# Retention heads: query, gate, key, gate as the order of the next head's first products, and the key groups moved with it

## The chip, the cores and the metric

The program runs on one core of one Trainium2 chip. The metric is the device time of one execution in microseconds (us). The kernel before took 2175.74 us, the median of three runs (2175.48 to 2181.7). The execution that the profiler recorded took 2178.27 us, of which 2176.5 us are the span of the trace.

## What is computed

The reference is one step of a decoder layer for 1024 prompt tokens and 8 sample tokens. The change touches only the part that does two things at once: the four retention heads of both groups, and the attention of the sample tokens over a paged cache of 4096 past tokens each.

```python
rq, rk, rv, rg, fq, fk, fv, ff, ga, gb = jnp.split(x @ w_in, offsets, axis=-1)
rq = rotary(rq.reshape(b, t, RET_HEADS, RET_DK), pos)
rk = rotary(rk.reshape(b, t, RET_HEADS, RET_DK), pos) * (RET_DK ** -0.5)
...
# per retention head, chunk by chunk (rq, rk, rv -> o, state)
inner = jnp.einsum('bihd,bjhd->bhij', qc, kc) * intra
o = einsum(inner, vc) + einsum(qc * q_decay, s)
...
rn = group_norm(ret_o) * gn_w + gn_b
u_a = (jax.nn.silu(rg) * rn) @ w_pa
merged = jax.nn.sigmoid(ga) * u_a + jax.nn.sigmoid(gb) * u_b
...
# sample tokens: softmax(q . k_past + bias) . v_past over 32 pages of 128 rows per token
```

## The kernel before

**Products.** One head needs ten products of the 1032 token columns with 128 columns of `w_in`: rotated query (rq), rotated key (rk), two gate tiles (ga), two value tiles (rv), two further gate tiles (gb) and two tiles of rg. They are numbered w = 0 to 9; `COLS` and `STEP` (L774, L775) give each its columns. A product (L108 to L126) has three chunks of 344 tokens, one PSUM bank each (banks 0, 1, 2), and a chunk is 24 matmuls: eight k-tiles times three terms, since weight and x are split in a high and a low part. TensorE starts a chunk only when the chunk of the product before it has been read out of its bank (`bank_free`), and starts a product only when its weight has been split: ScalarE makes the high part (L97), VectorE the low part (L104), and GpSimd reloads the raw weight slot after that (L89). There are two weight slots.

**Heads.** The first four products of head 0 stand before the loop (the opening). Products 4 to 9 of a head stand in its body, and at its end follow the first four products of the next head, called 10 to 13 here (the transition). There are three transitions. The head-to-head order of every engine is written out by hand.

**Who empties the banks.** A rotation (`rotate`, L1259 to L1270) is VectorE's: it reads the chunk's bank three times and writes `rq_t` or `rk_t`; it uses the two tiles `rot_cos` and `rot_sin`. A gate (`gate_chunk`, L1072 to L1079) is ScalarE's: a sigmoid from the bank into a tile `sg`, which is `rot_cos` or `rot_sin` again, and a store of 172 KB to DRAM. So gates wait until the rotations are through (L1085, L1177). The silu of rg (L1102) writes six buffers `silus`: the same two tiles and, for the other four, halves of `inner_t` and `q_decayed_t`. VectorE multiplies them into the normed output (L1376, six "gated products"), and ScalarE stores that (L1106).

**The cache stream.** While the heads run, the sample attention goes through 8 tokens, each with 16 groups of two pages of keys (VectorE: a multiply, L1199, and a reduction, L1203) and 16 groups of values (TensorE: 16 small matmuls, L913). Keys and values have four slots of 512 KB each. SyncE issues all loads in one fixed order, key group i of one token and then value group i of the token before, four such pairs to a pass of a loop; at the start of a pass it fetches the page numbers of the whole pass into registers. It issues key group i only when VectorE has reduced group i - 4 of that slot, and value group i only when TensorE has used group i - 4. The tables `VALUES_...` and `KEYS_...` (L691 to L700) say how many groups each engine takes at each place; `VALUES_B` and `KEYS_B` belong to the stretch from the norm to the end of the transition. After its last group a token goes through `cache_max`, a maximum over partitions on GpSimd, `cache_shift` (L1224), exp (L1070), and at the end `cache_tail` (L920, L924) on TensorE, `cache_norm` (L1232, L1234) on VectorE, `cache_turn` (L930) on TensorE and `cache_out`.

## Time and profile before

| | |
|---|---|
| median of the runs | 2175.74 us |
| the profiled execution | 2178.27 us, span 2176.5 us |
| the four heads, with opening and cache attention | about 370 to 1081 us |
| opening (first four products, first sample token's keys) | 372 to 428 us |
| first, second, third transition (products 10 to 13) | 544.51 to 609.80, 720.39 to 784.11, 894.38 to 957.76 us |
| TensorE busy, whole span | 1999.7 us (92%) |
| VectorE busy, whole span | 1158.6 us (53%) |

Times of rows are us from the start of the span, and durations are us unless marked ns. A row of the timeline has start, duration, engine, line, operation, output and inputs; in brackets stands how long the engine was idle before it and what it waited for. "SPq" rows are loads being issued by SyncE, one for both pages of a group (x2).

### The profile page before, as it was taken

What the parts mean: (1) busy time and instruction counts of PE and PEld (TensorE: products, weight loads), DVE (VectorE), ACT (ScalarE), POOL (GpSimd) and SP (SyncE); (2) the same over time, 40 slices, a digit from 0 to 9 for tenths busy, and PEclk for the clock granted to TensorE, in tenths of its full rate; (3) what the DMA queues carried; (4) which work ended last, traced back from release to release, by engine and by line L of the source; (5) the groups of instructions that cost most, each with busy time, mean ns of one, the idle gap of its engine ahead of it and who ended that gap; (6) DMA issues with size and microseconds to landing.
All of it is one profiled execution on the core that took longest, in us unless ns stands there. A gap on an engine that the chain in (4) does not pass through costs nothing.

```text
span 2176.5 us, 39095 instructions
## 1 busy us (share of the span) xinstructions
PE 1999.7 (92%) x14335; PEld 1868.4 (86%) x14335; DVE 1158.6 (53%) x1771; ACT 647.7 (30%) x1178; POOL 216.3 (10%) x253
## 2 busy tenths in 40 slices
PE   7998998898899799799798999799999999999996
PEld 5896887887798698698688898699999999999996
DVE  3654454967856866876332865733322333233348
ACT  4444443134123123223311101444301332123224
POOL 1000000020010020020000100400000001000004
PEclk9998999999899899899889999899999999999999
DMA  3211102597887877787742411111111111111154
GB/s 119 67 36 44 39 20 92 191 315 248 272 296 248 267 263 269 258 291 240 229 147 94 121 49 29 30 48 39 49 48 49 48 39 49 48 49 39 42 150 129
DMA packets 152256, 277.55 MB, mean 128 GB/s; under 512 B 19105, under 2 KB 58398, under 8 KB 152118
## 3 DMA queue, kind: packets, MB, share of 16 engines
q1 hardware_dynamic: 116114, 175.78, 24.3%
q0 software_dynamic: 23232, 82.80, 12.9%
q10 hardware_dynamic: 12800, 17.40, 2.2%
q8 instruction: 80, 1.31, 0.2%
q14 instruction: 30, 0.25, 0.0%
HBM read 247.77 MB, written 28.25 MB: 127 GB/s over the span
## 4 chain that ended last, share of the span: by engine, by line
PE 43%; DVE 5%; DMA 1%; issue 1%; ACT 1%; DVEq 0%; SPq 0%; ACTq 0%
PE bank L121 39%; PE bank L1624 3%; DVE x_lo L1845 1%; DMA gated_raw<-gated_t_scratch 1%; DVE chunk_tmp L1774 0%; DVE chunk_tmp L1776 0%; DVE z L1842 0%; PE banks L1582 0%; DVE merged_hi L1778 0%; DVE moving_lo L1780 0%; DVE w_lo L1915 0%; DMA tail_raw<-in_w_down_dram 0%; DVE y L1891 0%; DMA z<-fox_t_scratch 0%; PE banks L1610 0%
## 5 line engine op out<-in xcount | busy, mean ns | idle before, releaser
L121 PE MATMUL bank<-x_hi,w_hi 128*128 128x344 f32 (+1 forms) x1944 | 642.6, 331 | 55.1 <-DVE rot_sin L1267 25.2
L121 PE MATMUL bank<-x_lo,w_hi 128*128 128x344 f32 (+1 forms) x1944 | 632.2, 325 | 0.0
L121 PE MATMUL bank<-x_hi,w_lo 128*128 128x344 f32 (+1 forms) x1944 | 631.9, 325 | 0.0
L121 PEld LDWEIGHTS bank<-x_hi,w_hi 128*128 128x128 f32 (+1 forms) x1944 | 373.0, 192 | 73.7 <-issue 62.9
L121 PEld LDWEIGHTS bank<-x_lo,w_hi 128*128 128x128 f32 (+1 forms) x1944 | 372.8, 192 | 1.6
L121 PEld LDWEIGHTS bank<-x_hi,w_lo 128*128 128x128 f32 (+1 forms) x1944 | 372.7, 192 | 1.7
L97 ACT ACTIVATE w_hi<-w_raw 128x1024 fp32r<-128x1024 f32 (+3 forms) x139 | 141.7, 1022 | 550.1 <-PE bank L121 372.4
L121 PE MATMUL bank<-moving_hi,w_hi 128*128 128x344 f32 x744 | 229.8, 331 | 25.8 <-DVE moving_lo L1756 14.1
L121 PE MATMUL bank<-moving_lo,w_hi 128*128 128x344 f32 x744 | 239.6, 322 | 0.0
L104 DVE TENSOR_TENSOR w_lo<-w_raw,w_hi 128x1024 fp32r<-128x1024 f32 (+3 forms) x139 | 164.4, 1183 | 117.1 <-ACT w_hi L97 115.8
L121 PE MATMUL bank<-moving_hi,w_lo 128*128 128x344 f32 x648 | 210.0, 324 | 0.0
L1199 DVE TENSOR_TENSOR cache_keys<-cache_keys,q_wide 128x1024 f32<-128x1024 f32 x128 | 156.1, 1221 | 39.0 <-DMA cache_keys<-in_cache_k_dram 39.0
L121 PEld LDWEIGHTS bank<-moving_hi,w_hi 128*128 128x128 f32 x744 | 139.0, 192 | 35.3 <-issue 16.4
L1203 DVE TENSOR_REDUCE score<-cache_keys 128x16 f32<-128x1024 f32 x128 | 154.9, 1211 | 0.0
L121 PEld LDWEIGHTS bank<-moving_lo,w_hi 128*128 128x128 f32 x744 | 141.4, 190 | 0.1
L138 PE MATMUL bank<-x_hi,w_hi 128*128 128x344 f32 x384 | 138.0, 359 | 2.3 <-DVE rv_rows L1366 2.3
L1859 DVE SCALAR_TENSOR_TENSOR stage<-stage,conv_cols_tile 128x1024 f32<-128x1024 f32 x22 | 28.3, 1285 | 186.0 <-ACT stage L1699 186.0
L121 PEld LDWEIGHTS bank<-moving_hi,w_lo 128*128 128x128 f32 x648 | 124.4, 192 | 0.0
L138 PE MATMUL bank<-x_hi,w_lo 128*128 128x344 f32 x384 | 123.1, 321 | 0.0
L138 PE MATMUL bank<-x_lo,w_hi 128*128 128x344 f32 x384 | 122.8, 320 | 0.0
L89 POOL DMA_DIRECT2D w_raw<-in_w_in_dram x53 | 49.9, 943 | 651.6 <-DVE w_lo L104 520.8
L913 PE MATMUL bank<-cache_vals,score 128*2 128x128 f32 x2048 | 78.4, 275 | 28.5 <-DMA cache_vals<-in_cache_v_dram 25.9
(270 smaller groups left out, 2782.5 us busy)
## 6 DMA issues: line engine op xcount, KB each, us to landing
cache_keys<-in_cache_k_dram SPq DMA_DIRECT2D x256, 256.0 KB, 4.6
cache_vals<-in_cache_v_dram SPq DMA_DIRECT2D x256, 256.0 KB, 5.0
w_raw<-in_w_in_dram POOLq DMA_DIRECT2D x52, 512.0 KB, 5.6
w_raw<-in_w_up_dram POOLq DMA_DIRECT2D x22, 512.0 KB, 4.5
w_raw<-in_w_gate_dram POOLq DMA_DIRECT2D x22, 512.0 KB, 4.5
tail_raw<-in_w_down_dram SPq DMA_DIRECT2D x22, 448.0 KB, 3.9
gate<-gate_t_scratch SPq DMA_DIRECT2D x16, 516.0 KB, 3.5
w_raw<-in_w_down_dram POOLq DMA_DIRECT2D x10, 448.0 KB, 4.4
```

The costliest lines, as they stand in the source:

```text
L89: eng.dma_start(g.w_raw[slot][:, 0:kt, 0:m], src).then_inc(g.w_land[slot], 16)
L97: act.activation(g.w_hi[slot][:, 0:kt, 0:m], g.w_raw[slot][:, 0:kt, 0:m], ACT.Copy).then_inc(g.w_rounded, 1)
L104: dve.tensor_tensor(g.w_lo[slot][:, 0:kt, 0:m], g.w_raw[slot][:, 0:kt, 0:m], g.w_hi[slot][:, 0:kt, 0:m].bitcast(F32), ALU.subtract).then_i ...
L121: mm = pe.matmul(g.bank[n][0:m, 0:TC], w[slot][:, k, 0:m], x[:, k, chunk(n)], start=(k == 0 and i == 0), stop=(k == kt - 1 and i == 2))
L138: mm = pe.matmul(g.bank[n][0:m, 0:TC], w[slot][:, k, 0:m], x[:, k, chunk(n)], start=(k == 0 and q == 0), stop=(k == kt - 1 and q == 2))
L913: mm = pe.matmul(bank[7][32 * j:32 * j + 2, 0:P], score[u][:, i * GRP + p, 2 * j:2 * j + 2], vals[slot][:, p, j * P:(j + 1) * P], start=(f ...
L1199: dve.tensor_tensor(keys[slot][:], keys[slot][:], qb[u][:].unsqueeze(1).to_broadcast([P, GRP, FH * HD]), ALU.mult).then_inc(k_mult, 1)
L1203: dve.tensor_reduce(score[u][:, (i - 1) * GRP:i * GRP, :], keys[slot][:].rearrange("p g (h e) -> p g h e", e=HD), AX.X, ALU.add).then_inc( ...
L1624: mm = pe.matmul(bank[i % NCH][:, 0:hi - lo], w[slot][:, k, :], x[:, k, lo:hi], start=(k == 0 and q == 0), stop=(k == KT - 1 and q == 2))
L1845: dve.scalar_tensor_tensor(g.xl[:, k, chunk(n)], z[:, k, chunk(n)], ln_cols[:, 1, k:k + 1], g.xh[:, k, chunk(n)].bitcast(F32), ALU.add, AL ...
L1859: dve.scalar_tensor_tensor(act_in[:, 0:SEQ], up[:, 1:1 + SEQ], fc[:, 17:18], act_in[:, 0:SEQ], ALU.mult, ALU.add).then_inc(conv, 1)
```

## The change

In all heads and in the opening the first four products are taken in the order rq, ga, rk, ga. With it:

- `gate_chunk` gets a buffer to write into: for these six gates of a head it is `silus[2]` to `silus[5]` in turn, that is halves of `inner_t` and `q_decayed_t`, and no longer `rot_cos` and `rot_sin`. In place of the wait for the rotations stands one for the head's gated products (`gated`). GpSimd and VectorE, which write `q_decayed_t` and `inner_t` in the next head, wait for the stores of the gates.
- On ScalarE the high part of the weight of product 11 is made before the two stores of the gated output, not after them.
- On VectorE `KEYS_B` has new places: four groups before the gated products and none between them, two before the first rotation, one after each rotation of rq, five between rq and rk, one after the first and the second rotation of rk.
- On TensorE the value group that stood ahead of product 10 stands behind its first chunk, the groups behind the next chunks move on by one, and `cache_tail` and `cache_turn` stand one chunk earlier: behind the first and the second chunk of product 13.

```diff
--- before.py
+++ after.py
@@ -694,10 +694,10 @@
 KEYS_A_LAST = (1, 2, 1, 1, 2, 1) + (0, 1, 1, 0, 1, 1, 0, 1, 1) + (1, 0, 1, 0, 0, 0, 0)
 
 
-VALUES_B = (1,) + (1, 1, 1) + (1,) + (1,) * 9 + (2,)
+VALUES_B = (1,) + (1, 1, 1) + (0,) + (1, 1, 1, 1, 1, 1, 1, 1, 2) + (2,)
 VALUES_B_LAST = (1, 2, 2, 3) + (2,) + (1, 1, 1) + (3,)
 
-KEYS_B = (1,) + (1, 0, 1, 0) + (1,) + (1,) * 6 + (1,) * 6
+KEYS_B = (4, 2) + (1, 1, 1) + (5,) + (1, 1, 0)
 assert all(sum(s) == NG for s in (VALUES_A, KEYS_A, VALUES_A_LAST, KEYS_A_LAST, VALUES_B, VALUES_B_LAST, KEYS_B))
 
 
@@ -771,8 +771,8 @@
         NJ = 10
         IN, QDEC = slice(0, P), slice(P, 2 * P)
         KDEC, CDEC, RDEC = (slice(2 * P + i, 2 * P + i + 1) for i in range(3))
-        COLS = (C_RQ, C_RK, C_GA, C_GA + P, C_RV, C_RV + P, C_GB, C_GB + P, C_RG, C_RG + P)
-        STEP = (DK, DK) + (DV,) * 8
+        COLS = (C_RQ, C_GA, C_RK, C_GA + P, C_RV, C_RV + P, C_GB, C_GB + P, C_RG, C_RG + P)
+        STEP = (DK, DV, DK, DV) + (DV,) * 6
         NB = QB + 1
 
         def heads(eng, body):
@@ -874,6 +874,8 @@
                     pool.dma_start(st_s[:], a["state_ret"].rearrange("a b h d e -> d (a h) b e")[:, ds(h, 1)].rearrange("d a b e -> d (a b) e")).then_inc(s_land, 16)
                     pool.wait_ge(hc_land, h * 48 + 48)
                     pool.wait_ge(rot, h * 6 + 3)
+                    for b in range(2):
+                        wait_apart(pool, gate_stored[b], h * 96 + 49, g.mm_chunk)
                     for t in range(QB):
                         ins = pool.tensor_tensor(qd[:, t, :], rqT[:, t * P:(t + 1) * P], hc[:, QDEC], ALU.mult)
                     ins.then_inc(qd_done, 1)
@@ -946,11 +948,11 @@
 
                     def ending(n):
 
-                        if n == 0 and not last:
-                            values_b(14)
+                        if n == 0:
+                            if not last:
+                                values_b(14)
+                            cache_tail(h * 2 + 1, 1)
                         elif n == 1:
-                            cache_tail(h * 2 + 1, 1)
-                        elif n == 2:
                             cache_turn(h * 2 + 1)
 
                     def parts(w, of):
@@ -1069,24 +1071,26 @@
                     act.wait_ge(shifted, n + 1)
                     act.activation(score[u][:], score[u][:], ACT.Exp).then_inc(prob, 1)
 
-                def gate_chunk(j, i, h, tile, n):
+                def gate_chunk(j, i, h, tile, n, kept=None):
 
                     b = i % 2
                     act.wait_ge(gate_stored[b], h * 96 + (16 * (i // 2) + 1))
                     chunk_ready(g, act, j, n)
-                    act.activation(sg[b][:], bank[n][:, 0:TC], ACT.Sigmoid).then_inc(g.bank_free[n], 1)
+                    kept = sg[b][:] if kept is None else kept
+                    act.activation(kept, bank[n][:, 0:TC], ACT.Sigmoid).then_inc(g.bank_free[n], 1)
                     act.wait_ge(g.bank_free[n], j + 2)
-                    act.dma_start(g.gate_dram[ds(tile, 1), :, chunk(n)].rearrange("a p t -> (a p) t"), sg[b][:]).then_inc(gate_stored[b], 16)
+                    act.dma_start(g.gate_dram[ds(tile, 1), :, chunk(n)].rearrange("a p t -> (a p) t"), kept).then_inc(gate_stored[b], 16)
 
                 for b in range(2):
                     act.nop().then_inc(gate_stored[b], 1)
                 split_hi(g, act, job(J0, 1, 1))
                 split_hi(g, act, job(J0, 1, 2))
-                act.wait_ge(rot, 6)
-                for b in range(2):
-                    split_hi(g, act, job(J0, 1, 3 + b))
-                    for n in range(NCH):
-                        gate_chunk(J0 + 2 + b, 3 * b + n, 0, b, n)
+                for n in range(NCH):
+                    gate_chunk(J0 + 1, n, 0, 0, n, silus[2 + n % 4])
+                split_hi(g, act, job(J0, 1, 3))
+                split_hi(g, act, job(J0, 1, 4))
+                for n in range(NCH):
+                    gate_chunk(J0 + 3, 3 + n, 0, 1, n, silus[2 + (3 + n) % 4])
                 cache_exp(0, 0)
 
                 def body(h, last):
@@ -1169,16 +1173,19 @@
                         silu(3)
                         silu(4)
                     silu(5)
+                    if not last:
+                        nxt(NJ)
                     store_gated(0)
                     store_gated(1)
                     if not last:
-                        nxt(NJ)
                         nxt(NJ + 1)
-                        act.wait_ge(rot, h * 6 + 12)
-                        for b in range(2):
-                            nxt(NJ + 2 + b)
-                            for n in range(NCH):
-                                gate_chunk(h * NJ + (J0 + NJ + 2 + b), 12 + 3 * b + n, h, h * 2 + (2 + b), n)
+                        act.wait_ge(gated, (h + 1) * 6)
+                        for n in range(NCH):
+                            gate_chunk(h * NJ + (J0 + NJ + 1), 12 + n, h, h * 2 + 2, n, silus[2 + n % 4])
+                        nxt(NJ + 2)
+                        nxt(NJ + 3)
+                        for n in range(NCH):
+                            gate_chunk(h * NJ + (J0 + NJ + 3), 15 + n, h, h * 2 + 3, n, silus[2 + (3 + n) % 4])
                         cache_exp(h * 2 + 2, 0)
                 heads(act, body)
                 act.wait_ge(g_stored, RH * 32)
@@ -1273,9 +1280,9 @@
                     if w:
                         split_lo(g, dve, job(J0, 1, w + 1))
                     for n in range(NCH):
-                        if w < 2:
-                            rotate(J0 + w, 0, w, n)
-                        elif n == 2:
+                        if w != 1:
+                            rotate(J0 + w, 0, w // 2, n)
+                        if w == 2 and n == 2:
                             split_lo(g, dve, job(J0, 1, 4))
                         for i in share(NG, 9, 3 * w + n):
                             cache_logits(0, 0, i)
@@ -1305,6 +1312,9 @@
                     nxt(7)
                     for t in range(QB):
                         b = bank[4 + t % 2]
+                        if t == 0:
+                            for u in range(2):
+                                dve.wait_ge(gate_stored[u], h * 96 + 49)
                         dve.wait_ge(ik, h * QB + t + 1)
                         dve.tensor_tensor(inner[:, t, :], b[:, 0:P], hc[:, IN], ALU.mult).then_inc(ik_out, 1)
                         if t == 0:
@@ -1366,22 +1376,25 @@
                         dve.tensor_scalar(vrows[0:n, t, :], vrows[0:n, t, :], mv[0:n, t, 0:1], rstd[0:n, t:t + 1], ALU.subtract, ALU.mult).then_inc(gnd, 1)
                     nxt(9)
                     cache_sum(h * 2 + 1, 1)
-                    for k in range(6):
-                        keys_b(k)
+                    keys_b(0)
                     for w in (8, 9):
                         for n in range(NCH):
                             k = 3 * (w - 8) + n
                             dve.wait_ge(g.bank_free[n], h * NJ + J0 + w + 2)
                             dve.wait_ge(rn_out, (h + 1) * 2 * NB)
                             dve.tensor_tensor(rvT[:, w - 8, chunk(n)], rvT[:, w - 8, chunk(n)], silus[k] if k >= 2 else silus[k][:], ALU.mult).then_inc(gated, 1)
-                            keys_b(6 + k)
                     if not last:
-                        for w in range(2):
-                            nxt(NJ + w)
-                            for n in range(NCH):
-                                rotate(h * NJ + (J0 + NJ + w), h * 6 + 6, w, n)
-                                keys_b(12 + 3 * w + n)
+                        nxt(NJ)
+                        keys_b(1)
+                        for n in range(NCH):
+                            rotate(h * NJ + (J0 + NJ), h * 6 + 6, 0, n)
+                            keys_b(2 + n)
+                        nxt(NJ + 1)
+                        keys_b(5)
                         nxt(NJ + 2)
+                        for n in range(NCH):
+                            rotate(h * NJ + (J0 + NJ + 2), h * 6 + 6, 1, n)
+                            keys_b(6 + n)
                         cache_max(h * 2 + 2, 0)
                         nxt(NJ + 3)
                         cache_shift(h * 2 + 2, 0)
```

VectorE, from the end of the reductions before the gated products (`rv_t<-rv_t,...`) on, before:

```order
L1376 TENSOR_TENSOR rv_t<-rv_t,rot_cos 128x344
L1199 TENSOR_TENSOR cache_keys<-cache_keys,q_wide 128x1024
L1203 TENSOR_REDUCE score<-cache_keys 128x16
L1376 TENSOR_TENSOR rv_t<-rv_t,rot_sin 128x344
L1199 TENSOR_TENSOR cache_keys<-cache_keys,q_wide 128x1024
L1203 TENSOR_REDUCE score<-cache_keys 128x16
L1376 TENSOR_TENSOR rv_t<-rv_t,inner_t 128x344
```

VectorE at the same place now, up to the first rotation of the query:

```order
L1385 TENSOR_TENSOR rv_t<-rv_t,rot_cos 128x344
L1385 TENSOR_TENSOR rv_t<-rv_t,rot_sin 128x344
L1385 TENSOR_TENSOR rv_t<-rv_t,inner_t 128x344 x2
L1385 TENSOR_TENSOR rv_t<-rv_t,q_decayed_t 128x344 x2
L104 TENSOR_TENSOR w_lo<-w_raw,w_hi 128x1024
L1206 TENSOR_TENSOR cache_keys<-cache_keys,q_wide 128x1024
L1210 TENSOR_REDUCE score<-cache_keys 128x16
L1206 TENSOR_TENSOR cache_keys<-cache_keys,q_wide 128x1024
L1210 TENSOR_REDUCE score<-cache_keys 128x16
L1271 SCALAR_TENSOR_TENSOR rot_cos<-bank,cos 128x344
```

The six key groups that stood between and behind the gated products are gone from there; two of them stand behind the split of product 11's weight, the others later.

TensorE at the end of the transition (the last rows of product 13's first chunk, then `cache_tail`), before, with the semaphores that a row waits for:

```order
L913 MATMUL bank<-cache_vals,score 2x128 [waits v_land3]
L913 MATMUL bank<-cache_vals,score 2x128 x7
L121 MATMUL bank<-x_hi,w_hi 128x344 [waits bank_free1]
...
L920 MATMUL bank<-v_new,score 2x128 x4
L924 MATMUL bank<-ones_col,cache_prob_sum 2x1 [waits dec_summed]
L924 MATMUL bank<-ones_col,cache_prob_sum 2x1 x3
L121 MATMUL bank<-x_hi,w_hi 128x344 [waits bank_free2]
...
L930 MATMUL bank<-ident,dec_out 128x128 [waits dec_normed]
```

And now:

```order
L915 MATMUL bank<-cache_vals,score 2x128 [waits v_land3]
L915 MATMUL bank<-cache_vals,score 2x128 x7
L922 MATMUL bank<-v_new,score 2x128 x4
L926 MATMUL bank<-ones_col,cache_prob_sum 2x1 [waits dec_summed]
L926 MATMUL bank<-ones_col,cache_prob_sum 2x1 x3
L121 MATMUL bank<-x_hi,w_hi 128x344 [waits bank_free1]
...
L932 MATMUL bank<-ident,dec_out 128x128 [waits dec_normed]
L121 MATMUL bank<-x_hi,w_hi 128x344 [waits bank_free2]
```

The transposition that waits for VectorE's `cache_norm` (`dec_normed`) stood behind all of product 13 and now has the product's third chunk behind it.

## Rows read from the trace of the kernel before

**Rows 1.** The page: busy us, share of the span and instructions of each engine.

```profile
PE 1999.7 (92%) x14335; PEld 1868.4 (86%) x14335; DVE 1158.6 (53%) x1771; ACT 647.7 (30%) x1178; POOL 216.3 (10%) x253
```

**Rows 2.** TensorE's waits, 370 to 1081 us: us in total, times, longest.

```profile
PE bank L913 <- DMA cache_vals<-in_cache_v_dram: 25.9, 12, 4.9
PE bank L121 <- DVE rot_sin L1267: 25.2, 7, 7.8
```

**Rows 3.** Timeline of TensorE in the first transition.

```profile
539.18 0.62 PE L913 MATMUL bank<-cache_vals,score 128*2 128x128 f32 x16
...
543.96 0.62 PE L913 MATMUL bank<-cache_vals,score 128*2 128x128 f32 x16 [4.16 <-DMA cache_vals<-in_cache_v_dram]
...
550.57 0.43 PE L121 MATMUL bank<-x_hi,w_hi 128*128 128x344 f32 x1
...
555.10 0.42 PE L121 MATMUL bank<-x_hi,w_hi 128*128 128x344 f32 x1
...
567.49 0.63 PE L121 MATMUL bank<-x_hi,w_hi 128*128 128x344 f32 x1 [7.80 <-DVE rot_sin L1267]
...
609.80 0.27 PE L930 MATMUL bank<-ident,dec_out 128*128 128x128 f32 x1
```

**Rows 4.** Stretches: busy us of each engine, PEclk, DMA share, GB/s.

```profile
544.40:548.00 3.60, 3.60 (x20) 3.50 (x13) 2.47 (x4) 0.00 (x0) 0.00 (x0) 0.53 0.99 351
```

**Rows 5.** Groups of VectorE, 534 to 600 us: count, busy, mean ns, idle before.

```profile
L1199 DVE TENSOR_TENSOR cache_keys<-cache_keys,q_wide 128x1024 f32<-128x1024 f32 x16 | 19.4, 1219 | 5.8 <-DMA cache_keys<-in_cache_k_dram 5.8
```

**Rows 6.** Timeline of VectorE, first transition.

```profile
534.36 1.21 DVE L1199 TENSOR_TENSOR cache_keys<-cache_keys,q_wide 128x1024 f32<-128x1024 f32 x1
...
558.06 1.23 DVE L1199 TENSOR_TENSOR cache_keys<-cache_keys,q_wide 128x1024 f32<-128x1024 f32 x1 [3.30 <-DMA cache_keys<-in_cache_k_dram]
...
562.24 1.23 DVE L1199 TENSOR_TENSOR cache_keys<-cache_keys,q_wide 128x1024 f32<-128x1024 f32 x1 [1.40 <-DMA cache_keys<-in_cache_k_dram]
...
564.51 1.21 DVE L104 TENSOR_TENSOR w_lo<-w_raw,w_hi 128x1024 fp32r<-128x1024 f32 x1
565.76 0.52 DVE L1264 SCALAR_TENSOR_TENSOR rot_cos<-bank,cos 128x344 f32<-128x344 f32 x1
...
567.81 1.22 DVE L1199 TENSOR_TENSOR cache_keys<-cache_keys,q_wide 128x1024 f32<-128x1024 f32 x1
```

**Rows 7.** Timeline of VectorE, end of the first transition.

```profile
593.90 1.22 DVE L1203 TENSOR_REDUCE score<-cache_keys 128x16 f32<-128x1024 f32 x1
...
599.31 0.43 DVE L1224 TENSOR_TENSOR score<-score,cache_max_all 128x264 f32<-128x264 f32 x1
606.05 0.17 DVE L1232 RECIPROCAL dec_inv<-bank 128x1 f32<-128x1 f32 x1 [6.32 <-PE bank L924]
```

**Rows 8.** Timeline of SyncE's issues, first transition.

```profile
538.02 1.97 SPq L809 DMA_DIRECT2D cache_keys<-in_cache_k_dram  x2
...
546.97 0.85 SPq L809 DMA_DIRECT2D cache_vals<-in_cache_v_dram  x2
554.64 1.02 SPq L809 DMA_DIRECT2D cache_keys<-in_cache_k_dram  x2
...
557.08 0.85 SPq L809 DMA_DIRECT2D cache_keys<-in_cache_k_dram  x2
```

**Rows 9.** Timeline of ScalarE, first transition.

```profile
549.42 11.82 ACTq L1106 DMA_DIRECT2D gated_t_scratch<-rv_t  x2
561.34 2.00 ACT L97 ACTIVATE w_hi<-w_raw 128x1024 fp32r<-128x1024 f32 x2 [21.09 <-DVE rv_t L1376]
```

**Rows 10.** Timelines of TensorE, then VectorE, then SyncE, opening.

```profile
440.44 0.40 PE L913 MATMUL bank<-cache_vals,score 128*2 128x128 f32 x8 [2.66 <-DMA cache_vals<-in_cache_v_dram]
456.23 0.40 PE L913 MATMUL bank<-cache_vals,score 128*2 128x128 f32 x8 [2.18 <-DMA cache_vals<-in_cache_v_dram]
...
424.14 1.23 DVE L1199 TENSOR_TENSOR cache_keys<-cache_keys,q_wide 128x1024 f32<-128x1024 f32 x1 [2.69 <-DMA cache_keys<-in_cache_k_dram]
...
435.33 0.85 SPq L809 DMA_DIRECT2D cache_vals<-in_cache_v_dram  x2
```

## The prediction

> **What bounds the kernel now.** I read first the busy times of the page [rows 1]: TensorE has 92% of the span, so a change pays only where TensorE stands still or runs at the lower clock. Then TensorE's waits over the four heads [rows 2]: the two large ones are values that have not landed, 25.9 us, and banks that a rotation still has to empty, 25.2 us in 7 waits. Then the timeline of a transition [rows 3]. It has one wait of each kind: 4.16 us ahead of product 10, for a value group, and 7.80 us ahead of product 11, for the first rotation. The reader is to see that both stand in front of whole products, and that the three transitions repeat it (value waits of 4.16, 4.92, 4.12 us, rotation waits of 7.80, 5.66, 4.92; one transition is shown). Behind each, TensorE's granted clock is 0.53, nearly all of it at 1.2 and not 2.4 GHz [rows 4]: the chunk that began at 544.51 took to 550.57, 6.06 us with its value group, the next one 4.53 [rows 3]. So a long wait costs 1.5 us more in the chunk behind it; the rotation wait, whose chunk had the low clock for longer, about 1.9. In one transition that makes 12.0 + 3.4 = 15.4 us. Last I read who is late: VectorE [rows 5 to 7] and, behind it, SyncE [rows 8].
>
> **What VectorE has to do there.** Its order begins with the first key group at 534.36 [rows 6] and ends with the shift at 599.31 to 599.74 [rows 7]. In it lie 16 key groups of 1.13 + 1.13 us (a row has 1.22 [rows 5], but the starts stand 1.13 apart, as 564.51 behind 562.24 shows for two of them [rows 6]), 36.2; six rotations of 2.05 (565.76 to 567.81 [rows 6]), 12.3; four splits at 1.13 to 1.25, 4.8; six gated products at 0.43, 2.6; and the tail, from the last reduction at 593.90 on, 5.8 with its wait but without that reduction 4.7 [rows 7]. That is about 59 us, and 5.8 us of waits for keys [rows 5]. The change leaves the work as it is. It moves it, so VectorE can end earlier only by its waits.
>
> **The transition with the change, step by step** (first transition, by its own clock; all instructions keep their durations).
> 1. Product 10 starts at 539.8, when value group 3 is done (539.18 and 0.62 [rows 3]), and no longer waits for value group 4; that one landed at 543.9 and is now wanted at 543.7. The 4.16 and the 1.5 behind it go.
> 2. VectorE: four key groups to 542.3 as before, six gated products to 544.9, split of product 11 to 546.0 (its high part was made at 561.34 before [rows 9], behind the two stores; now it can be made at 540.3). Then two key groups to 550.6, and the first rotation frees bank 0 at 552.2. TensorE comes to product 11 at 539.8 + 3 x 4.53 = 553.4. The wait of 7.80 goes, and its 1.9.
> 3. Rotations 2 and 3 free their banks at 556.5 and 560.8; TensorE wants them only for the key product, and product 11's chunks want them at 558.0 and 562.5. No wait. The gates of products 11 and 13 are ScalarE's (a sigmoid of 0.46 us), in buffers of their own; ScalarE is idle here (21.09 us before the row in [rows 9]).
> 4. Keys. SyncE issues key group 7 only when group 3 is reduced. That is at 548.4, and no longer 545.1, since the gated products and the split now stand before it. Value 7 follows, and then the gap in which the page numbers are fetched: 547.82 to 554.64 before [rows 8], 6.8 us. So key group 8 goes from 554.6 to 557.3, and lands 3.4 later (554.64 to 558.06 [rows 6, 8]), at 560.7; it is wanted at 561.3. Group 11 waits for the reduction of group 7 (563.6) and goes out at 564.1, value 11 at 565.2; with the gap, group 12 goes out at 572.6 and lands at 576.0. Group 13, in the middle of a burst, lands 5.2 after its issue at 574.9 (557.08 to 562.24 [rows 6, 8]), at 580.1.
> 5. VectorE would want group 12 at 571.5, since five groups now stand between rotations. It waits 4.5 and then 1.8 us. Here the old wait comes back: 6.3 us in place of 5.8. Split of product 13 to 583.5; the first rotation of rk frees bank 0 at 585.1, and TensorE, there at about 582, waits 3 us.
> 6. Two rotations, two key groups, the last reduction at 594.2, the tail of 5.4 to the shift's start: 599.6, end 600.0, `cache_norm` to 600.7.
> 7. TensorE has product 13's second chunk done by 594 to 596 and stands before `cache_turn` until 600.7. It has been idle five us, so I take the low clock for the third chunk: 3.8 + 1.9 = 5.7. The end is 606.4, and 609.80 before [rows 3]: 3.4 us gained.
>
> So of 15.4 us about 12 come back as waits behind VectorE: before, `cache_norm` waited 6.32 us for TensorE [rows 7], now TensorE waits for it. Three transitions give 10.2.
>
> **The opening.** The same order, and VectorE's table of keys is unchanged. The rotations of rk come later by three chunks. VectorE's wait of 2.69 us [rows 10] goes in part (group 12 is issued earlier), a smaller one appears at group 8: the keys end 0.8 us sooner. The first value group is now limited by the exp behind them, 438.9 in place of 440.44. SyncE can issue it from 432.4 and not 435.33, so the wait of 2.18 at 456.23, also for a value, shrinks to 0.7 [rows 10]. Gain 3.0; bounds 0 (nothing reaches the value group at 456.23) and 4.8 (both value waits go).
>
> **Small edits.** The waits on `gate_stored` ahead of `inner_t` and `q_decayed_t`: the stores are issued by 607 and the next head writes these tiles 20 us later and more; nothing, and if that cover were gone at most a store's few us. The stores of the gated output (516 KB each) go out at 543.7 and 545 and not at 549.42 and 560.8 [rows 9], into a stretch where the DMA share is already 0.99 at 351 GB/s [rows 4]. 1 MB at that rate is 3 us of the engines. Value groups 4 and 5 and key groups 5 to 7 are in flight then; group 6 would land at 551.8 and is wanted at 552.6. I take nothing; bounds 0 and 3 us per transition. The Trainium skill (DMA: Bandwidth & Descriptors, "Issuing engines are not separate DMA queues") says that transfers of all issuing engines end on the same 16 engines and interleave, so that a second issuing engine saves only issue time. The trace of before cannot show this case, as both stores lie in other places there. By the rule the 3 us fall on the keys; by the row nothing waits for them yet. By the rule alone the sum would be 9 us smaller.
>
> **The sum.** 3.0 + 3 x 3.4 = 13.2. The profiled execution took 2178.27, so 2165.1; the median of the runs is 2.5 below it, so 2162.5. Bounds: VectorE without any wait for keys ends at 593.7, TensorE at 600.1, 9.7 per transition. VectorE with the 3 us of the stores on top: 0.4 per transition.
>
> **Rivals.**
> A. The keys come in time. If the gap between two passes is hidden or landing takes 3.4 in every case, VectorE does not wait and 9.7 x 3 + 3 = 32 us are gained, 2144. For it: landings of 3.4 [rows 6, 8]. Against: the gap before each pass is there whatever VectorE does, and its waits add up to 5.8 already [rows 5].
> B. It is given back in full. The moved stores and the later group 7 add 3 us to VectorE's waits: 0.4 per transition, gain about 3 in all, 2173. For it: the DMA share of 0.99 [rows 4]. Against: the groups concerned have slack of 0.6 to 4 us in step 4.
> C. Slower. Since `cache_turn` stands ahead of the third chunk, each us that VectorE is late beyond 600.0 is one of TensorE. Landing counts twice: a late group 8 delays the reduction of group 7, with it the issue of group 11 and, behind the gap, of group 12. If groups land 9 us after issue and not 3.4 to 5.2, group 8 is there at 566.3, group 11 goes out at 568.6, group 12 at 577.1 and lands at 586.1, 14.6 after it is wanted in place of 6.3 for both waits. The transition ends at 614.7, 4.9 lost; three times that less the opening's 3 is 11.7 slower, 2187. It decides from a landing of about 7 us on, where VectorE is 4.4 later than in step 5 (the 3.4 and the opening's share). For it: five groups in a row at the densest place. Against: no landing in these rows is over 5.2.
>
> **How the numbers follow.** The forecast, a gain of 7 to 20, has 0.57: 2156 to 2169. A 0.13, B 0.19, C 0.11. A measurement tells 0.3% (6.5 us) from no change. Faster: forecast and A and a small part of B, 0.71; same 0.19; slower 0.10. The range takes in B up to 2174 and A down to 2147; what is left out is most of C and the far end of A, somewhat under 2 in 10.
>
> **What would show it.** In the trace of after, no value wait before product 10 and no rotation wait before product 11, and the first at full clock (step 1, 2). VectorE's longest wait for keys in a transition at group 12, 4 to 5 us, just behind the pass's gap on SyncE (4, 5). A wait of some 3 us at the first rotation of rk. A wait of 4 to 6 us of TensorE for `dec_out` in all three transitions, with low clock behind it (7), and VectorE's shift 65 us after its first key group as before. If TensorE's wait for `dec_out` is below 1 us, A holds. If the transition, from value group 3 to `cache_turn` plus one chunk, is 70 us as before, B.

## The result, and the profile after

The changed kernel took 2164.62 us, the median of four runs (2160.85 to 2168.46), beside 2177.51 (2175.48 to 2181.7) for the kernel before, run beside it: a ratio of 0.9942, 95% interval 0.9919 to 0.9964. That is 13 us, 0.6%. The execution that was profiled took 2168.46, of which 2166.8 are its span. A second set of six runs (c_after below) gave 2163.68 and a ratio of 0.9935 (0.9921 to 0.9948) to its own set of the kernel before.

The page's busy times are those of [rows 1], so the gain is idle time and clock:

```profile
PE 1999.5 (92%) x14335; PEld 1868.4 (86%) x14335; DVE 1159.0 (53%) x1771; ACT 648.4 (30%) x1178; POOL 221.3 (10%) x253
```

TensorE's and VectorE's waits, 370 to 1071 us (engine, what waited, for whom: us in total, times, longest), answer to [rows 2]:

```profile
DVE cache_keys L1206 <- DMA cache_keys<-in_cache_k_dram: 39.4, 27, 3.6
PE bank L932 <- DVE dec_out L1241: 17.7, 7, 5.5
PE bank L915 <- DMA cache_vals<-in_cache_v_dram: 15.8, 12, 3.5
PE bank L121 <- DVE rot_sin L1274: 10.0, 6, 3.1
```

Values and rotations held TensorE for 51.1 us before and hold it for 25.8 now. A row that had 1.1 us in the same window before, the wait for `dec_out`, has 17.7. The reader is to see that two thirds of what the edit freed stand in one new row. The same trade is seen from VectorE's side. Before, in that window, VectorE waited for TensorE at the token's end, and waited as long for keys as now; the last row is the changed kernel's:

```profile
DVE dec_inv L1232 <- PE bank L924: 18.9, 3, 6.3
DVE cache_keys L1199 <- DMA cache_keys<-in_cache_k_dram: 39.0, 25, 5.1
...
DVE dec_inv L1239 <- PE bank L926: 0.9, 1, 0.9
```

TensorE in the first transition, to be laid beside [rows 3] (before, product 10 started at 539.8; now at 537.99):

```profile
541.96 0.62 PE L915 MATMUL bank<-cache_vals,score 128*2 128x128 f32 x16
...
553.60 0.62 PE L915 MATMUL bank<-cache_vals,score 128*2 128x128 f32 x16 [2.54 <-DMA cache_vals<-in_cache_v_dram]
...
583.70 0.40 PE L121 MATMUL bank<-x_hi,w_hi 128*128 128x344 f32 x1 [0.40 <-DVE rot_sin L1274]
...
598.62 0.48 PE L932 MATMUL bank<-ident,dec_out 128*128 128x128 f32 x1 [5.49 <-DVE dec_out L1241]
```

Value group 4 comes at 541.96 without a wait. From the end of value group 3, where product 10 starts now, to the end of product 13 it was 70.0 us and is 66.5 (the next product starts at 604.44): 3.5 us gained of 15.4. VectorE at the same place [rows 5 to 7], its group over 532 to 600 us and then the waits:

```profile
L1206 DVE TENSOR_TENSOR cache_keys<-cache_keys,q_wide 128x1024 f32<-128x1024 f32 x16 | 19.4, 1218 | 6.2 <-DMA cache_keys<-in_cache_k_dram 6.2
```

```profile
565.77 1.23 DVE L1206 TENSOR_TENSOR cache_keys<-cache_keys,q_wide 128x1024 f32<-128x1024 f32 x1 [0.51 <-DMA cache_keys<-in_cache_k_dram]
...
569.94 1.22 DVE L1206 TENSOR_TENSOR cache_keys<-cache_keys,q_wide 128x1024 f32<-128x1024 f32 x1 [1.81 <-DMA cache_keys<-in_cache_k_dram]
...
574.70 1.23 DVE L1206 TENSOR_TENSOR cache_keys<-cache_keys,q_wide 128x1024 f32<-128x1024 f32 x1 [2.40 <-DMA cache_keys<-in_cache_k_dram]
...
578.57 1.23 DVE L1206 TENSOR_TENSOR cache_keys<-cache_keys,q_wide 128x1024 f32<-128x1024 f32 x1 [1.52 <-DMA cache_keys<-in_cache_k_dram]
...
597.67 0.43 DVE L1231 TENSOR_TENSOR score<-score,cache_max_all 128x264 f32<-128x264 f32 x1 [0.26 <-POOL cache_max_all L853]
```

The four waits are key groups 10 to 13. VectorE has the same work and about the same time of waits (6.2 us, 5.8 before), and TensorE now reaches the end of the token before it.

What SyncE, ScalarE's queue and GpSimd issue around 540 us ([rows 8, 9] before):

```profile
542.07 0.85 SPq L809 DMA_DIRECT2D cache_vals<-in_cache_v_dram  x2
546.71 0.89 SPq L809 DMA_DIRECT2D cache_keys<-in_cache_k_dram  x2
...
554.84 0.86 SPq L809 DMA_DIRECT2D cache_keys<-in_cache_k_dram  x2
...
541.90 1.61 ACTq L1110 DMA_DIRECT2D gated_t_scratch<-rv_t  x2
...
544.85 0.88 POOL L89 DMA_DIRECT2D w_raw<-in_w_in_dram  x1 [11.11 <-DVE w_lo L104]
```

and the stretches of it, columns as in [rows 4]:

```profile
546.00:554.00 8.00, 5.46 (x60) 4.65 (x58) 7.86 (x11) 1.06 (x1) 0.00 (x0) 1.00 1.00 375
554.00:558.00 4.00, 4.00 (x25) 3.85 (x17) 3.93 (x6) 0.00 (x0) 0.00 (x0) 0.63 0.48 158
558.00:570.00 12.00, 12.00 (x111) 10.66 (x110) 9.63 (x11) 2.87 (x5) 0.88 (x1) 0.98 0.96 345
```

The value group that TensorE waits for at 553.60 is number 6 (counted from 0), issued at 542.07: it took 11.5 us, in a stretch where the DMA engines are full (a share of 1.00 at 375 GB/s). Behind the wait the granted clock is 0.63 for 4 us.

In the opening both value waits of [rows 10] are gone. The first value group of the changed kernel comes 68.2 us after the first product's start, and 70.9 before:

```profile
440.40 0.62 PE L915 MATMUL bank<-cache_vals,score 128*2 128x128 f32 x16
```

**A cleaner measure.** The start of the heads lies anywhere between 364 and 374 us in the profiled executions, and that scatter is as large as the effects looked for here. So beside the medians each kernel gets its heads' length in the profiled execution: from the first chunk of the first product to the first chunk behind the cache's last token. In the changed kernel these are

```profile
372.19 0.62 PE L121 MATMUL bank<-x_hi,w_hi 128*128 128x344 f32 x1 [2.62 <-PEq L422]
...
1077.99 0.62 PE L121 MATMUL bank<-moving_hi,w_hi 128*128 128x344 f32 x1 [10.28 <-DVE moving_lo L1769]
```

705.8 us. Before it was 369.49 to 1087.60, 718.1. The kernels ran in sets, each with its own runs of the kernel before, so kernels of different sets are best compared by their ratios. All runs:

| kernel | median, us | ratio to before, 95% | heads, us |
|---|---|---|---|
| before (three sets of runs) | 2176.74, 2176.08, 2176.69 | 1 | 718.1 |
| changed | 2164.62 | 0.9942 [0.9919, 0.9964] | 705.8 |
| changed, again (c_after) | 2163.68 | 0.9935 [0.9921, 0.9948] | 706.2 |
| e_turn_late | 2147.40 | 0.9869 [0.9849, 0.9888] | 685.0 |
| e_value_ahead | 2161.76 | 0.9932 [0.9912, 0.9953] | 704.1 |
| e_ids_spread | 2197.30 | 1.0099 [1.0083, 1.0114] | 734.9 |
| e_five_first | 2163.79 | 0.9937 [0.9917, 0.9957] | 703.3 |
| e_turn_next | 2145.96 | 0.9862 [0.9841, 0.9882] | 687.6 |
| e_next_five | 2146.25 | 0.9863 [0.9840, 0.9885] | 683.8 |
| e_old_order | 2162.73 | 0.9946 [0.9926, 0.9966] | 704.3 |
| e_next_one_fetch (leaves out the choice of pages) | 2129.46 | 0.9794 [0.9773, 0.9814] | 676.3 |
| e_next_prefetch | 2140.06 | 0.9828 [0.9810, 0.9847] | 680.7 |
| e_next_five_prefetch | 2141.44 | 0.9855 [0.9834, 0.9876] | 682.0 |
| e_stores_late | 2160.61 | 0.9930 [0.9914, 0.9946] | 706.0 |

One execution of e_turn_next took 4302.46 us and is left out of its ratio, but not of its median, which would be 2145.06 without it.

### The profile page after: what moved, and what is told of

Read it like the earlier page. It is cut to its first block, busy times and chain, and to the rows that moved or that the text cites. A ratio compares the mean times of both kernels' runs of the same rounds, so it can differ in the third digit from the quotient of the medians.

```text
span 2166.8 us, 39107 instructions
## 1 busy us (share of the span) xinstructions
PE 1999.5 (92%) x14335; PEld 1868.4 (86%) x14335; DVE 1159.0 (53%) x1771; ACT 648.4 (30%) x1178; POOL 221.3 (10%) x253
## 4 chain that ended last, share of the span: by engine, by line
PE 43%; DVE 5%; DMA 1%; issue 1%; ACT 1%; SPq 0%; DVEq 0%; ACTq 0%
PE bank L121 39%; PE bank L1637 3%; DVE x_lo L1858 1%; DMA gated_raw<-gated_t_scratch 1%; DVE chunk_tmp L1787 0%; DVE chunk_tmp L1789 0%; DVE z L1855 0%; PE banks L1595 0%; DVE merged_hi L1791 0%; DVE moving_lo L1793 0%; DVE w_lo L1928 0%; DMA tail_raw<-in_w_down_dram 0%; DVE y L1904 0%; DMA z<-fox_t_scratch 0%; PE banks L1623 0%
## 5 line engine op out<-in xcount | busy, mean ns | idle before, releaser
L121 PE MATMUL bank<-x_hi,w_hi 128*128 128x344 f32 (+1 forms) x1944 | 641.4, 330 | 40.7 <-DVE x_lo L1858 15.7
```

What stands on the lines that cost most here:

```text
L121: mm = pe.matmul(g.bank[n][0:m, 0:TC], w[slot][:, k, 0:m], x[:, k, chunk(n)], start=(k == 0 and i == 0), stop=(k == kt - 1 and i == 2))
```

## The experiments

**c_after.** The changed kernel once more, in one set with the three that follow.

> The changed kernel once more, as the control of the others. Both theories: some 13 us faster than before (ratio 0.994), with a wait of TensorE for dec_out of 5 us in the first two transitions and 3 in the third.

2163.68, `dec_out` 15.7 us in 6 waits, values 15.3 in 11. The time and the new row are there again. Inside the heads the second execution differs from the first: TensorE waits 16.3 us for rotations and not 10.0, and the first transition takes 69.1 us and not 66.5. Its VectorE waits for keys four times there, 8.8 us in all; two of the four waits (the groups 6 and 12), and two issues ahead of the first:

```profile
537.90 1.01 SPq L809 DMA_DIRECT2D cache_keys<-in_cache_k_dram  x2
538.12 1.61 ACTq L1110 DMA_DIRECT2D gated_t_scratch<-rv_t  x2
...
549.34 1.23 DVE L1206 TENSOR_TENSOR cache_keys<-cache_keys,q_wide 128x1024 f32<-128x1024 f32 x1 [2.14 <-DMA cache_keys<-in_cache_k_dram]
...
573.24 1.22 DVE L1206 TENSOR_TENSOR cache_keys<-cache_keys,q_wide 128x1024 f32<-128x1024 f32 x1 [4.23 <-DMA cache_keys<-in_cache_k_dram]
```

Key group 6 was issued at 537.90, just ahead of the stores of the gated output, and was there 11.4 us later. All three transitions of the two executions, from the end of value group 3 to the start of the next head's product 4, with VectorE's waits for keys:

| | first | second | third | sum |
|---|---|---|---|---|
| before | 70.0 (5.8) | 69.6 (5.6) | 68.5 (4.1) | 208.1 |
| changed | 66.5 (6.2) | 65.6 (5.6) | 68.3 (8.3) | 200.3 |
| changed, again | 69.1 (8.8) | 68.0 (7.1) | 67.1 (7.0) | 204.2 |

In the six transitions of the changed kernel the length without VectorE's waits for keys is 59.9 to 60.9 us, and VectorE's shift starts 53.4 to 53.6 us after product 10 plus these waits. So what differs from transition to transition is how long VectorE waits for keys, and TensorE's own waits on the way do not show in the sum.

**e_turn_late.** Who is late at the end of a token?

```
-  elif n == 1:
+  elif n == 2:
       cache_turn(h * 2 + 1)
```

> The changed kernel with cache_turn behind the third chunk of product 13 and no longer behind the second. Theory V (VectorE's chain sets the moment of the transposition, and only its place on TensorE costs): the third chunk runs in the time that is waited now, at full clock; the waits of 5.5, 5.2 and 3.2 us shrink to 2, 1.5 and 0, and the low clock behind them goes. 3.8 + 1.9 us per transition, 13 to 17 us faster than the changed kernel. Rival D (the next head's first product waits for something else that is late too, the split of its weight, its banks or the values): under 5 us faster.

```profile
598.37 0.33 PE L932 MATMUL bank<-ident,dec_out 128*128 128x128 f32 x1 [0.99 <-DVE dec_out L1241]
```

```profile
PE bank L932 <- DVE dec_out L1241: 5.4, 5, 1.8
```

16 us by the medians, 14 by the ratios, 21 by the heads. `cache_turn` runs at the same time as in the changed kernel (598.37 and 598.62, with product 10 started at 537.72 and 537.99), but the whole third chunk of product 13 has gone by before it. VectorE's waits for keys in this transition are 6.1 us, as in the changed kernel (6.2). So the new wait was real, and it stood one chunk too early: TensorE had work beside it that the order did not let it do.

**e_value_ahead.** Does it matter that the value group moved from ahead of product 10 to behind its first chunk?

```
-VALUES_B = (1,) + (1, 1, 1) + (0,) + (1, 1, 1, 1, 1, 1, 1, 1, 2) + (2,)
+VALUES_B = (1,) + (1, 1, 1) + (1,) + (1,) * 9 + (2,)
```

> The changed kernel with one value group ahead of product 10 as before. Theory V: the value wait of some 4 us comes back with low clock behind it, but TensorE has that much room until it stands before VectorE's dec_out, which stays where it is: 0 to 3 us slower in all than the changed kernel, and the waits for dec_out shrink. Rival W (the value wait and its clock were worth their full length): 3 x 5.7 = 17 us slower than the changed kernel, about as slow as before or slower.

```profile
PE bank L915 <- DMA cache_vals<-in_cache_v_dram: 19.6, 9, 4.1
PE bank L932 <- DVE dec_out L1241: 13.4, 6, 3.5
```

The wait for values is back (3.84 us at 538.35), the waits for `dec_out` are shorter (3.5 us in the first transition and not 5.5), and the time is the same. A wait that TensorE had before product 10 is worth nothing as long as VectorE ends the transition.

**e_ids_spread.** SyncE fetches the page numbers of each pair just ahead of its loads, and not sixteen at the start of a pass.

```
-  key_ids, value_ids = page_ids(n + 1, q), page_ids(n, q)
   for slot in range(SLOTS):
-      load_group(keys, ..., key_ids); load_group(vals, ..., value_ids)
+      load_group(keys, ..., pair_ids(n + 1, q, slot))
+      load_group(vals, ..., pair_ids(n, q, slot))
```

> The changed kernel with SyncE fetching the page numbers of one group just ahead of its load, in place of all sixteen at the start of a pass; the same loads in the same order. Theory S (the gap of 6 to 7 us at a pass's start makes VectorE's waits for keys): issues come about 2.8 us apart without a gap, the waits for keys of a transition fall from 6.2 to under 3 us, dec_out comes 3 to 4 us sooner, 9 to 15 us faster than the changed kernel. Rival B (the DMA engines are full, the keys land late whatever SyncE does): within 3 us of the changed kernel, the waits for keys stay at 6 per transition.

A miss. The kernel is 34 us slower than the changed one. Its SyncE:

```profile
570.71 0.86 SPq L809 DMA_DIRECT2D cache_keys<-in_cache_k_dram  x2
573.10 0.85 SPq L809 DMA_DIRECT2D cache_vals<-in_cache_v_dram  x2
575.33 0.85 SPq L809 DMA_DIRECT2D cache_keys<-in_cache_k_dram  x2
```

A pair takes 4.6 us, and 2.2 to 2.4 without a fetch ([rows 8], 554.64 to 557.08). In the changed kernel the pass from key group 8 to 12 took 15.7 us (554.84 to 570.54); spread it is 4 x 4.6 = 18.4. VectorE's work for four of sixteen groups is 59 / 4 = 14.8, an estimate from the transition's 59 us. VectorE's waits for keys went from 42.5 us (c_after) to 79.7, TensorE's for values from 15.3 to 37.3. The loads themselves landed sooner, 3.5 us after their issue in the median over the heads and not 4.9, so the DMA engines are not what was slow. What it showed by missing: in a transition SyncE's own instructions are as long as VectorE's work, so neither theory of where the fetch stands was complete without what it costs.

**e_five_first.** Five key groups ahead of the gated products, one behind, so that key group 7 and value group 7 go out earlier.

```
-KEYS_B = (4, 2) + (1, 1, 1) + (5,) + (1, 1, 0)
+KEYS_B = (5, 1) + (1, 1, 1) + (5,) + (1, 1, 0)
...                       # VectorE, ahead of the rotations of rq
+dve.wait_ge(gated, (h + 1) * 6)
```

> The changed kernel with five key groups in place of four before the gated products, and one in place of two before the first rotation. Theory S (SyncE's order is what VectorE and TensorE wait for: key group 7 and with it value group 7 and everything behind it go out only when key group 3 is reduced, and the reduction of group 4 now stands ahead of the gated products, so groups 7 and 8 go out earlier): value group 7 is issued 2 to 5 us earlier, TensorE's waits for it (2.54, 2.42, 1.64 us in the three transitions) fall below 0.5 and the low clock behind them goes, VectorE ends 1 to 3 us sooner and TensorE waits that much less for dec_out: 3 to 9 us faster than the changed kernel, 2155 to 2161. Theory D (the 16 DMA engines are full from 558 us on, at a share of 0.96, so that what is issued earlier lands no earlier): value group 7's wait goes, but the later key groups land as before and the waits for dec_out stay at 5.5, 5.2, 3.2: within 3 us of the changed kernel, or 1 to 3 faster.

```profile
550.06 0.62 PE L915 MATMUL bank<-cache_vals,score 128*2 128x128 f32 x16
...
581.55 0.62 PE L121 MATMUL bank<-x_hi,w_hi 128*128 128x344 f32 x1 [3.04 <-DVE rot_sin L1274]
...
596.48 0.47 PE L932 MATMUL bank<-ident,dec_out 128*128 128x128 f32 x1 [4.01 <-DVE dec_out L1241]
```

The added wait is for VectorE's own gated products, which stand ahead of it anyway. The 2.54 us are gone, but not for the reason that theory S gives. The expectation calls the late group number 7; counted in the trace it is 6 (550.06 here), whose issue does not hang on key group 3. The likely reason is that the gated products, and with them the stores, now come behind its issue (540.73, the stores at 543.04) and not beside it (542.07 and 541.90); that the stores can do this is shown by e_stores_late. In its place stand 3.04 us at the first rotation of rk, the wait that the prediction had named there. 2163.79: no change. That is the time that theory D gives, but not by full DMA engines (e_next_one_fetch below); what fixed it was VectorE's end: its two waits for keys there, 3.63 and 1.75 us, are 5.4 where the four were 6.2.

**e_turn_next.** `cache_turn` behind the first chunk of the next head's product 4.

```
   for w in (4, 5):
-      product(..., after=lambda n, w=w: values_a(3 * (w - 4) + n))
+      product(..., after=lambda n, w=w: head_start(w, n))   # cache_turn at w == 4, n == 0
```

The last head has no next one; there the transposition stands behind the third chunk.

> The changed kernel with cache_turn moved out of product 13, to behind the first chunk of the next head's product 4. Theory V (what the new order left is TensorE's wait for VectorE's end of the token): with the turn behind the third chunk of product 13 there were still waits of 0.99, 1.79 and 1.25 us; these go, and the time is 14 to 20 us below the changed kernel, 2144 to 2150. Rival G (the place matters no more once the wait is short, and the copy of dec_out then delays product 4's own work): the same as with the turn behind the third chunk, 2147 to 2152.

2145.96, within 2 us of e_turn_late (heads 687.6 and 685.0): rival G. `dec_out` is down to 1.3 us in all, but the first transition has 2.88 at value group 6 and 3.15 at rk's first rotation. Once TensorE no longer waits at the end, it arrives earlier at the next place where VectorE or SyncE is late.

**e_next_five.** Both edits.

> The changed kernel with both: cache_turn in the next head, and five key groups before the gated products. Theory V with S: the gains add, 17 to 28 us below the changed kernel, 2136 to 2147. Theory V with D (or if VectorE's end no longer reaches TensorE, so that only value group 7's wait is left to gain): 2 to 5 us below the kernel with cache_turn alone moved.

2146.25, as with cache_turn alone (ratios 0.9863 and 0.9862; heads 683.8 and 687.6). The gains do not add. V with D had 2 to 5 us below the kernel with cache_turn alone; the heads show 3.8, the medians nothing. TensorE's waits for values fell from 18.1 to 7.9 us over the heads, and those for rotations rose from 9.2 to 19.0: the one went into the other.

**e_old_order.** The order of the products as before (rq, rk, ga, ga, gates in `rot_cos` and `rot_sin`), with the rest of the change.

```
 COLS, STEP, gate_chunk, rotate, gate_stored waits: as before
-KEYS_B = (4, 2) + (1, 1, 1) + (5,) + (1, 1, 0)
+KEYS_B = (4, 2) + (1, 1, 1) + (1,) + (1, 1, 4)
```

> The order of the products as before the change (rq, rk, ga, ga; gates in rot_cos and rot_sin, waiting for all rotations), but with the rest of the change: the value group moved behind product 10's first chunk, the high part of product 11's weight before the stores, the gated products in one piece, cache_tail and cache_turn one chunk earlier; key groups four before the gated products, two before the first rotation, one after each of the three rotations of rq, one behind the low part of rk's... three rotations, and four behind the last. Theory K (the gain came from the early gated products and from moving key groups behind the rotations; the gates in between are not needed): within 3 us of the changed kernel, 2161 to 2168. Rival O (the gate product between the two rotated ones is what gives VectorE time: without it TensorE waits for each rotation of rk for 3 us or more per transition): at least 8 us slower than the changed kernel, 2172 or more, about as the kernel before.

```profile
551.61 0.62 PE L913 MATMUL bank<-cache_vals,score 128*2 128x128 f32 x16 [2.38 <-DMA cache_vals<-in_cache_v_dram]
...
585.76 0.66 PE L121 MATMUL bank<-x_hi,w_hi 128*128 128x344 f32 x1 [4.46 <-DVE w_lo L104]
```

2162.73, as the changed kernel: theory K. The gates between the rotations are not what gained. No rotation is waited for in this transition; in its place TensorE waits 4.46 us for the low part of product 13's weight, which VectorE makes late, and `dec_out` is ready when it comes. The two orders differ in where they are fast: up to the first `cache_turn` this kernel needs 154.7 us from the heads' start, as before (154.4), and the changed one 149.9 (148.5 in its second execution); from there on it needs 549.6 and the changed one 555.9 (557.7). Its transitions take 66.2, 66.1 and 66.1 us, with 2.6, 2.9 and 2.3 us of waits for keys. So the new order of the products pays in the opening, and in the transitions the rest of the change does at least as much without it. For the opening more executions speak: the twelve with the new order need 147.6 to 151.8 us to the first `cache_turn`, the two with the old one 154.4 and 154.7.

**e_next_one_fetch.** On the kernel with cache_turn in the next head: what do the page numbers cost? SyncE fetches them once, so that every pass reads the same pages. This leaves out the choice of pages by the table.

```
+fixed_keys, fixed_values = page_ids(1, 0), page_ids(0, 0)
 def period(n):
     with sp.Fori(0, NG // SLOTS) as q:
-        key_ids, value_ids = page_ids(n + 1, q), page_ids(n, q)
```

> The kernel with cache_turn in the next head, and SyncE fetching page numbers only once, before all passes (left out: the choice of pages by the table, so that every pass reads the same eight pages of keys and of values; bytes, loads and waits are as before). Theory P (the 6.8 us gap in which SyncE fetches 16 page numbers at the start of each pass is what makes keys and values late): SyncE's issues follow each other without the gap, value group 7's wait (2.88 in the first transition) and VectorE's waits at groups 12 and 13 (3.64 and 3.15) fall below 1 us, and with them TensorE's wait at the first rotation of rk (3.15): 15 to 30 us below the kernel with cache_turn alone moved (2145.96), 2116 to 2131. Theory D (the DMA engines are full there: a share of 0.95 to 1.00 at 300 to 375 GB/s): the groups are issued earlier and land no earlier; the waits for keys stay at 6 us or more per transition, and the time is within 6 us of it, 2140 to 2150.

```profile
560.73 0.85 SPq L809 DMA_DIRECT2D cache_keys<-in_cache_k_dram  x2
561.83 0.85 SPq L809 DMA_DIRECT2D cache_vals<-in_cache_v_dram  x2
565.04 1.59 SPq L809 DMA_DIRECT2D cache_keys<-in_cache_k_dram  x2
566.88 0.85 SPq L809 DMA_DIRECT2D cache_vals<-in_cache_v_dram  x2
```

```profile
DVE cache_keys L1212 <- DMA cache_keys<-in_cache_k_dram: 17.0, 17, 2.5
```

2129.46, 16.5 us below e_turn_next (14.8 by the ratios, 11.3 by the heads). VectorE's waits for keys in the first transition fall from 9.3 to 2.8 us, over all heads from 40.9 to 17.0, and rk's first rotation is no longer waited for there. Theory P holds, at the low end of its range; "the DMA engines are full" does not, since as many bytes came in time. That the loads gain from reading the same pages again is not seen: over the heads a key load landed 5.0 us after its issue in the median, 4.8 in e_turn_next. The 40 us from some 7 us behind product 10's start on, in e_turn_next and then in this kernel:

```profile
540.00:580.00 40.00, 34.62 (x323) 30.53 (x322) 30.36 (x34) 5.83 (x7) 1.14 (x2) 1.00 0.90 316
548.00:588.00 40.00, 37.57 (x344) 33.91 (x344) 36.74 (x45) 5.83 (x7) 2.51 (x3) 1.00 1.02 357
```

The same 16 engines moved 357 GB/s in place of 316 once SyncE asked for more. Value group 6 is still waited for (2.43 at 556.65), which theory P had put below 1: that one is not the gap's.

**e_next_prefetch.** Nothing left out: the next pass's eight key numbers are fetched ahead of the fourth pair of a pass, the eight of the values behind the first key group.

```
 for q in range(NG // SLOTS):
     for slot in range(SLOTS):
+        if slot == SLOTS - 1 and q < NG // SLOTS - 1: next_ids = page_ids(n + 1, q + 1)
         load_group(keys, ..., key_ids)
+        if slot == 0: value_ids = page_ids(n, q)
         load_group(vals, ..., value_ids)
```

The four passes are written out here (`range` in place of the hardware loop `Fori`), a second difference that no run takes apart.

> The kernel with cache_turn in the next head, and the page numbers fetched at other places: the eight of the next pass's keys before the fourth pair of a pass (where SyncE waits 2 to 4 us for the slot anyway), the eight of the values behind the first key group. Nothing is left out. Theory P: most of the gap is gone in front of key group 12 (issue 3 to 6 us earlier), half of it stands in front of value group 12; 8 to 25 us below the kernel with cache_turn alone moved, 2121 to 2138, and somewhat above the one with a single fetch. Theory D: within 6 us of it, 2140 to 2150.

```profile
563.99 0.85 SPq L809 DMA_DIRECT2D cache_vals<-in_cache_v_dram  x2
565.08 0.92 SPq L809 DMA_DIRECT2D cache_keys<-in_cache_k_dram  x2
568.78 0.85 SPq L809 DMA_DIRECT2D cache_vals<-in_cache_v_dram  x2
```

The gap of 6 us is now one of 2.8 (566.00 to 568.78) behind a key group and another that falls where SyncE waits anyway. VectorE waits 6.0 us in the first transition and not 9.3, TensorE 0.59 at rk's first rotation and not 3.15. 2140.06, 6 us below e_turn_next, heads 6.9. By the time this is just inside theory D's range (2140 to 2150) and above P's; by the shorter waits it is P's mechanism with less of an effect. The intervals of the two ratios touch (0.9810 to 0.9847, 0.9841 to 0.9882), so the gain is probable and not certain. It is the fastest of the kernels that compute everything: 0.9828 of the kernel before, 37 us.

**e_next_five_prefetch.** With five key groups first.

> As the one before (cache_turn in the next head, page numbers fetched ahead), and five key groups ahead of the gated products, one behind. Theory P: key group 7 is issued before its slot is a bound, the value waits go as well; 0 to 6 us below the kernel with the page numbers ahead alone. Rival (VectorE's own work is the bound by then, so that it no longer matters where the groups stand): within 3 us of it, or a little slower, as product 11's first rotation then comes one group later.

2141.44, heads 682.0. The rival: the place of one key group no longer matters. Beside e_next_five (ratio 0.9863, heads 683.8) the early fetches bring little (0.9855, 682.0): VectorE waits 41.8 us for keys and not 35.2, TensorE 21.6 for values and not 7.9.

**e_stores_late.** The changed kernel with the stores of the gated output behind the gates of product 11.

```
-store_gated(0)
-store_gated(1)
 ...                      # gates of product 11, high parts of 12 and 13
+store_gated(0)
+store_gated(1)
```

> The changed kernel with the two stores of the gated output (516 KB each) moved behind the gates of product 11 and the high parts of products 12 and 13, to about 572 us. Rule R (transfers of all issuing engines share the same 16 DMA engines, so 1 MB beside the loads is 3 us that they come later): the landings at 546 to 558 us get up to 3 us shorter, value group 7's wait (2.54, 2.42, 1.64) falls by 1 to 2.5; but the same 3 us now meet key groups 12 and 13, whose waits rise: in sum within 4 us of the changed kernel. Rival N (the stores take nothing from anyone, or a place behind 570 is free): value group 7's wait and those for dec_out are as in the changed kernel, and the time within 2 us of it.

```profile
547.51 0.62 PE L915 MATMUL bank<-cache_vals,score 128*2 128x128 f32 x16
...
557.84 0.62 PE L915 MATMUL bank<-cache_vals,score 128*2 128x128 f32 x16 [1.24 <-DMA cache_vals<-in_cache_v_dram]
...
580.56 0.40 PE L121 MATMUL bank<-x_hi,w_hi 128*128 128x344 f32 x1 [3.17 <-DVE rot_sin L1275]
```

The stores go out at 576.09. Value group 6, issued at 538.19, is there at 547.51 without a wait: at most 9.3 us in place of 11.5. The Trainium skill (DMA: Bandwidth & Descriptors, "Issuing engines are not separate DMA queues") says that the transfers of all issuing engines interleave on the same 16 engines. This run agrees: the load came at least 2.2 us sooner, and 1 MB at 375 GB/s is 2.8 us. The sum is unchanged, 706.0 against 705.8 and 706.2, as rule R says. Its reason for that, longer waits for the key groups 12 and 13, does not show: they are 1.3 and 2.3 us here, 2.4 and 1.5 in the changed kernel, 4.2 and 1.7 in its second execution. VectorE's waits for keys in the first transition add up to 7.6 us, between the 6.2 and the 8.8 of those two, with five groups late instead of four. What TensorE saves at value group 6 (and 1.24 of it is back at value group 8) it waits at the first rotation.

## Why the prediction came out right

The forecast was 2162.5; it was 2164.62. Point by point, for the first transition of the execution that was profiled first, with the prediction's clock moved by the 1.8 us that product 10 started earlier (537.99 for 539.8):

1. Product 10 without a wait: so it was. Value group 4 was there at 541.96. (In the second execution it was 1.54 us late.)
2. The first rotation frees bank 0 at 550.4: it ended at about 550.4, and product 11 waited for no rotation. But product 11 did not start at full clock. **This is the step that failed**, and the sentence was "I take nothing; bounds 0 and 3 us per transition": value group 6, with a slack of 0.8 in the working, came 2.54 us late, and the low clock behind it made the chunk 1.5 us longer (5.59 for 4.04), 4.1 us together and so beyond the bound. The stores of 1 MB are at least 2.2 us of the wait (e_stores_late). Something else was not in the prediction at all: the early split of product 11 also frees the weight slot, and GpSimd reloads it at 544.85 and not at 566.29, half a megabyte more in the same place. No run moves this reload alone; in e_stores_late it is there too (540.31) and the group is in time, so its share is not shown.
3. No waits for rotations 2, 3 and the gates: right.
4. SyncE, in the shifted clock: key group 7 at 546.6, measured 546.71; group 12 issued 570.8, measured 570.54; landed 574.2, measured 574.70. Only group 8, at 555.5 by the sum and 554.84 in the trace, was ahead of it.
5. VectorE's waits: 6.3 forecast, 6.2 measured. Not as one of 4.5 and one of 1.8, but spread over groups 10 to 13, because groups 10 and 11 took 6.5 and 7.9 us from issue to landing (559.31 to 565.77, 562.03 to 569.94) and not 5.2. Group 12 sets the end either way. This is what rival C wanted, a landing of about 7 us; it touched two groups ahead of the one that decides, whose issue hangs on SyncE's pass. TensorE's 3 us at rk's first rotation were 0.40, since it came 3 us later, for point 2; in the second execution they were 2.61, and group 12 was waited for 4.23 us and group 13 1.71, the prediction's 4.5 and 1.8.
6. Shift at 597.8, measured 597.67.
7. 5 us of waiting for `dec_out`, measured 5.49; low clock behind it (5.69 us for the chunk, 5.7 forecast); end at 604.6, measured 604.44.

So in this execution the mis-sized store cost nothing in the sum: whatever held TensorE in the middle, VectorE ended the transition. The second execution shows that this need not be so. There the key group beside the stores was late by 2.14 us on VectorE (e_stores_late has no wait at that group), ahead of the two forecast waits, and the first transition ended at 69.1 us: 0.9 gained, close to rival B's 0.4. The mechanism (VectorE's chain and its waits for keys set the length) holds in all six transitions; that the first one met the forecast within 0.2 us is luck in part.

Two terms of the sum were off in size, in opposite directions. The opening gave 4.5 and 5.9 us in the two executions (154.4 to 149.9 and 148.5 up to the first `cache_turn`) and not 3.0; the second is beyond its bound of 4.8. The transitions gave 7.8 and 3.9 us and not 10.2, since the first transition stood for three and the waits for keys were taken as its own 6.3. The third had been 1.5 us shorter than the first before (its two waits were 9.04 us and not 11.96), and VectorE waits 8.3 and 7.0 us for keys in it. The heads gained 12.3 and 11.9 us in all, for 13.2; the parts vary more between the two executions (up to 3.9 us) than the whole (0.4), so the nearness of the whole is luck in part too. One slip had no effect: the listed work of VectorE adds up to 60.6 us and not 59, because the split at 598.17 is counted among the splits and in the tail; the rows give 599.31 - 534.36 - 5.8 = 59.1.

Of the rivals, A needed keys that come in time. No run gives these to the changed kernel itself; e_next_one_fetch shows that it is worth another 11 to 16 us once `cache_turn` is out of the way. B, the stores, was probably right that they can reach VectorE (group 6 in the second execution; no run isolates it) and wrong that this would take back the gain.

What stays open: whether the old order in the transitions with the new one in the opening would be better than both (not tried); what share of value group 6's wait is the weight's, and why the group is late in e_next_one_fetch; and why e_turn_late gains 21 us in the heads and 14 to 16 in the time.
